# A modulation stage rewritten: plain fp32 products of raw weight blocks in four column groups of TensorE

## The reference, cut to what matters

```python
def ada_modulation(c, w_ada, b_ada):
    return jnp.split(jax.nn.silu(c) @ w_ada + b_ada, N_MOD, axis=-1)

def trunk_layer(x, c, ...):
    shift1, scale1, gate1, shift2, scale2, gate2 = ada_modulation(c, w_ada, b_ada)
    h = modulate(rms_norm(x, g_norm1), shift1, scale1)      # h * (1 + scale) + shift
    ...                                                     # attention, S5, output projection, PEER experts
```

## Time and profile before

| | us |
|---|---|
| median of 3 runs | 5242.03 (5230.54 to 5265.98) |
| the profiled execution, its own time | 5261.86 |
| its span, first to last instruction | 5260.2 |
| end of the modulation products in that span (`scale1` is made) | 394.92 |

### The profile page before, as it was taken

The page is one execution under the profiler, slowest core; times in us unless marked ns, Lnnn a source line. Parts: engine busy times, 40 slices in busy tenths (PEclk is TensorE's granted clock), DMA queues, the critical chain, the costliest instruction groups (busy, mean ns, idle before and its releaser), DMA issues. The chain is left out here.

```text
span 5260.2 us, 58810 instructions
## 1 busy us (share of the span) xinstructions
PE 4319.6 (82%) x23026; PEld 3825.3 (73%) x23026; DVE 2787.5 (53%) x4247; ACT 1426.3 (27%) x1507; POOL 536.8 (10%) x461
## 2 busy tenths in 40 slices
PE   4677998674447989235499999999999999999997
PEld 2227997463336979234499999999989888888896
DVE  4663223316663232699744444444456667666675
ACT  4553112101232131057522222222222222222222
POOL 0000000005300000044300000000000000000000
PEclk8888998766678999667799999999999999999998
DMA  6762221222203222112476666666667667666764
GB/s 246 304 253 73 87 80 53 90 74 43 66 31 134 81 99 95 53 56 96 152 261 236 236 233 232 237 236 233 233 241 272 228 251 255 242 247 238 256 244 160
DMA packets 219977, 912.23 MB, mean 173 GB/s; under 512 B 23138, under 2 KB 111586, under 8 KB 137650
## 3 DMA queue, kind: packets, MB, share of 16 engines
q1 hardware_dynamic: 178018, 641.51, 33.8%
q0 software_dynamic: 37376, 268.52, 14.6%
q10 hardware_dynamic: 4432, 0.20, 0.1%
HBM read 818.10 MB, written 87.87 MB: 172 GB/s over the span
## 5 line engine op out<-in xcount | busy, mean ns | idle before, releaser
L2269 DVE TENSOR_TENSOR part_lo<-raw,part_hi 128x2048 fp32r<-128x2048 f32 x128 | 293.4, 2292 | 464.3 <-ACT part_hi L2191 464.3
L2191 ACT ACTIVATE part_hi<-raw 128x2048 fp32r<-128x2048 f32 x128 | 245.3, 1917 | 1050.4 <-PE ps_u L2231 489.7
L2269 DVE TENSOR_TENSOR h_lo<-raw,h_hi 128x2048 fp32r<-128x2048 f32 x128 | 293.4, 2292 | 388.6 <-ACT h_hi L2191 387.7
L2191 ACT ACTIVATE h_hi<-raw 128x2048 fp32r<-128x2048 f32 x128 | 245.3, 1916 | 925.0 <-PE ps_u L2231 475.8
L2246 PE MATMUL ps_v<-h_hi,part_hi 128*128 128x448 f32 x1024 | 384.6, 376 | 46.3 <-issue 41.0
L2231 PE MATMUL ps_u<-h_hi,part_hi 128*128 128x448 f32 x1024 | 378.0, 369 | 19.4 <-DVE part_lo L2269 19.4
L2246 PE MATMUL ps_v<-h_lo,part_hi 128*128 128x448 f32 x1024 | 382.2, 373 | 0.0
L2246 PE MATMUL ps_v<-h_hi,part_lo 128*128 128x448 f32 x1024 | 382.0, 373 | 0.0
L2231 PE MATMUL ps_u<-h_lo,part_hi 128*128 128x448 f32 x1024 | 377.8, 369 | 0.0
L2231 PE MATMUL ps_u<-h_hi,part_lo 128*128 128x448 f32 x1024 | 377.7, 369 | 0.0
L2231 PE MATMUL ps_u<-h_hi 128*128 128x448 f32 x1024 | 376.8, 368 | 0.0
(11 more groups left out here) (389 smaller groups left out, 9020.5 us busy)
## 6 DMA issues: line engine op xcount, KB each, us to landing
raw<-in_uT SPq DMA_DIRECT2D x128, 1024.0 KB
raw<-in_vT SPq DMA_DIRECT2D x128, 1024.0 KB
qkvu<-in_w_ada SPq DMA_DIRECT2D x48, 2048.0 KB, 8.3
w_raw<-in_w_in SPq DMA_DIRECT2D x32, 1024.0 KB
wo_raw<-in_w_out_q SPq DMA_DIRECT2D x32, 1024.0 KB, 4.9
gates_scratch<-gate_blk SPq DMA_DIRECT2D x14, 2048.0 KB, 7.5
a_scratch<-wt SPq DMA_DIRECT2D x128, 224.0 KB, 1.9
at<-a_scratch SPq DMA_DIRECT2D x16, 1792.0 KB, 7.6
```

The source lines that it names most:

```text
L2191: act.activation(hi[n % 2], raw[n % 2][:].rearrange("p (k c) -> p k c", k=KC), ACT.Copy).then_inc(hi_done, 1)
L2269: dve.tensor_tensor(lo[n % 2], raw[n % 2][:].rearrange("p (k c) -> p k c", k=KC), hi[n % 2].bitcast(F32), ALU.subtract).then_inc(lo_done, 1)
```

## The change

Only `modulate` changes, and one small constant input, `pick`, is added. The weights are no longer split. PE multiplies the raw fp32 halves as they land, as plain fp32. `c` has one set of columns: `c_cols`, 9 columns of silu(c) and 23 of zeros for each chunk. Chunk k's product is written to PSUM partitions 32*(k % 4) and on, so the 16 chunks of a block fall into four column groups with four partial sums. ACT copies all 128 x 512 partial sums; the turning is a plain fp32 product of that copy (as stationary operand, 128 columns at a time) with `pick`, a 128 x 9 matrix that adds the four groups; DVE adds the bias in one operation. The raw halves lie in a ring of four buffers, and SP reloads a buffer when PE has used it (`half_used`). All loops are written out instead of run as hardware loops. The diff, cut to its core:

```diff
-        raw = [free[:, u * KC * WB:(u + 1) * KC * WB].rearrange("p (k c) -> p k c", k=KC) for u in range(2)]
+        raw = [free[:, u * KC * WB // 2:(u + 1) * KC * WB // 2].rearrange("p (k c) -> p k c", k=KC // 2) for u in range(NR)]
...
+        c_cols = sb("c_cols", [P, KC, CG_])
+        pick = sb("pick", [P, NC_])
...
-        row = [sb(f"row{u}", [2 * NC_, WB]) for u in range(2)]
+        row = [sb(f"row{u}", [P, WB]) for u in range(2)]
...
-                for f in range(2):
-                    if not isinstance(n, int):
-                        sp.wait_ge(lo_done[f], n - 1)
...
+            def load(n):
+                if n >= NR:
+                    sp.wait_ge(half_used, n - NR + 1)
+                sp.dma_start(raw[n % NR].rearrange("p k c -> p (k c)"), w_ada[n // 2, n % 2]).then_inc(w_full[n % NR], 16)
+
+            load(0)
+            load(1)
             sp.dma_start(x[:], I["xT"].rearrange("(k p) t -> p k t", p=P)).then_inc(x_in, 16)
...
+            for n in range(2, 2 * NBLK):
+                load(n)
+
+        @block.gpsimd
+        def _(pool):
+            pool.memset(c_cols[:], 0.0).then_inc(cleared, 1)
...
+            act.dma_start(pick[:], I["pick"]).then_inc(small_in, 16)
+            act.wait_ge(small_in, 64)
+            act.wait_ge(cleared, 1)
+            act.activation(c_cols[:, :, 0:NC_], c_in[:], ACT.Silu).then_inc(silu_done, 1)
...
-            def high_parts(n, u, f):
-                act.wait_ge(w_full[u][f], 8 * (n - u) + 16)
-                act.wait_ge(used[f], n)
-                act.activation(w_hi[f], raw[u][:, f * KH:(f + 1) * KH, :], ACT.Copy).then_inc(hi_done[f], 1)
...
+            for n in range(NBLK):
+                act.wait_ge(half_used, 2 * n + 2)
+                if n >= 2:
+                    act.wait_ge(mod_t, n - 1)
+                act.activation(row[n % 2][:], ps_row[n % 2][:], ACT.Copy).then_inc(row_copied, 1)
...
+            def rows(n):
+                if n >= 2:
+                    pe.wait_ge(row_copied, n - 1)
                 for f in range(2):
-                    pe.wait_ge(lo_done[f], n + 1)
-                    for k in range(KH):
-                        for w in (w_hi, w_lo):
-                            mm = pe.matmul(ps_row[u][0:2 * NC_, :], c_two[:, f * KH + k, :], w[f][:, k, :],
...
+                    i = 2 * n + f
+                    pe.wait_ge(w_full[i % NR], 16 * (i // NR + 1))
+                    for k in range(KC // 2):
+                        g, part = k % CT, f * (KC // 2) + k
+                        mm = pe.matmul(ps_row[n % 2][g * CG_:(g + 1) * CG_, :], c_cols[:, part, :], raw[i % NR][:, k, :],
+                                       start=part < CT, stop=part >= KC - CT)
+                    mm.then_inc(half_used, 1)
+
+            def turn(n):
+                pe.wait_ge(row_copied, n + 1)
+                if n >= 2:
+                    pe.wait_ge(mod_done, n - 1)
+                for j in range(JB):
+                    mm = pe.matmul(ps_mod[n % 2][:, j * NC_:(j + 1) * NC_], row[n % 2][:, j * P:(j + 1) * P], pick[:],
+                                   start=True, stop=True)
+                mm.then_inc(mod_t, 1)
+
+            rows(0)
...
+            for n in range(1, NBLK):
+                rows(n)
+                turn(n - 1)
+            turn(NBLK - 1)
...
-            def low_parts(n, u, f):
-                dve.wait_ge(hi_done[f], n + 1)
-                dve.tensor_tensor(w_lo[f], raw[u][:, f * KH:(f + 1) * KH, :], w_hi[f].bitcast(F32),
-                                  ALU.subtract).then_inc(lo_done[f], 1)
...
+    a["pick"] = np.concatenate([np.eye(32, NC_, dtype=np.float32)] * 4)
```

More of the change, by code:

```diff
@@ L123, in modulate @@
     ps = lambda n, s, d=F32: ctx.enter_context(nc.psum_tensor(n, s, d))
-    KH = KC // 2
+    NBLK = NMOD * P // WB
+    CT, CG_ = 4, 32
+    KT = KC // CT
+    NR = 4
+    JB = WB // P
     with ctx:
@@ L146, in modulate @@
         ps_mod = [ps(f"ps_mod{u}", [P, 512]) for u in range(2)]
-        x_in, small_in, w_full = sem("x_in"), sem("small_in"), [[sem(f"ada_full{u}{f}") for f in range(2)]
-                                                                        for u in range(2)]
-        silu_done, c_hi_done, c_lo_done = sem("silu_done"), sem("c_hi_done"), sem("c_lo_done")
+        x_in, small_in, w_full = sem("x_in"), sem("small_in"), [sem(f"ada_full{u}") for u in range(NR)]
+        cleared, silu_done = sem("c_cleared"), sem("silu_done")
         sq_done, sq_used, norm_sum, std_done = (sem(n) for n in ("sq_done", "sq_used", "norm_sum", "std_done"))
[L152 to L157, removed]
+        half_used, row_copied, mod_t, mod_done = (sem(n) for n in ("ada_used", "row_copied", "mod_t", "mod_done"))
         xn_done, scale_done, h_prompt, h_sample = (sem(n) for n in ("xn_done", "scale_done", "h_prompt", "h_sample"))
         hin_done = sem("hin_hi_done"), sem("hin_lo_done")
-        held = sem("ada_held")
         v_step = sem("mod_v_step")
-        NA = NMOD * P // WB // 2
         block = ctx.enter_context(nc.Block())
[L165 to L180, removed]
         @block.sync
@@ L204, in _ @@
             act.dma_start(g1[:], I["g1T"]).then_inc(small_in, 16)
[L205 to L218, removed]
-            def high_parts(n, u, f):
-                act.wait_ge(w_full[u][f], 8 * (n - u) + 16)
-                act.wait_ge(used[f], n)
-                act.activation(w_hi[f], raw[u][:, f * KH:(f + 1) * KH, :], ACT.Copy).then_inc(hi_done[f], 1)
[L225 to L230, removed]
+            act.dma_start(pick[:], I["pick"]).then_inc(small_in, 16)
+            act.wait_ge(small_in, 64)
+            act.wait_ge(cleared, 1)
+            act.activation(c_cols[:, :, 0:NC_], c_in[:], ACT.Silu).then_inc(silu_done, 1)
+            act.wait_ge(x_in, 16)
+            for c in range(KC):
+                if c >= 2:
+                    act.wait_ge(sq_used, c - 1)
+                act.activation(sq[c % 2][:], x[:, c, :], ACT.Square).then_inc(sq_done, 1)
+            act.wait_ge(norm_sum, 1)
+            act.activation(halves(std[:]), fold(ps_norm), ACT.Sqrt, scale=1.0 / D, bias=C["eps"][:, 0:1]
+                           ).then_inc(std_done, 1)
+            for n in range(NBLK):
[3 more added lines that the diff above has]
+                act.activation(row[n % 2][:], ps_row[n % 2][:], ACT.Copy).then_inc(row_copied, 1)
             act.wait_ge(scale_done, 1)
@@ L244, in _ @@
         def _(pe):
[L245 to L255, removed]
@@ L270, in turn @@
[L270 to L286, removed]
@@ L287, in _ @@
-            turn(NA - 1, 0)
-            rows(2 * NA - 1, 1)
-            turn(NA - 1, 1)
+            pe.wait_ge(silu_done, 1)
+            def rows(n):
+                if n >= 2:
+                    pe.wait_ge(row_copied, n - 1)
+                for f in range(2):
+                    i = 2 * n + f
[5 more added lines that the diff above has]
+                    mm.then_inc(half_used, 1)
@@ new lines, in turn @@
+            def turn(n):
[7 more added lines that the diff above has]
+            rows(0)
+            for c in range(KC):
+                pe.wait_ge(sq_done, c + 1)
+                for a in range(2):
+                    mm = pe.matmul(ps_norm[:, a, 0:HT], C["ones"][:], sq[c % 2][:, a * HT:(a + 1) * HT],
+                                   start=(c == 0), stop=(c == KC - 1))
+                if c < KC - 1:
+                    mm.then_inc(sq_used, 1)
@@ L303, in keep @@
[L303 to L310, removed]
@@ L312, in norm, with keep @@
-            def norm():
-                dve.wait_ge(std_done, 1)
-                step(dve.reciprocal(rstd[:], std[:]))
-                for c in range(KC):
-                    ins = dve.tensor_tensor(x[:, c, :], x[:, c, :], rstd[:], ALU.mult)
-                    if c == KC - 1:
-                        ins.then_inc(xn_done, 1)
-                    else:
-                        step.mark(ins)
-                dve.wait_ge(small_in, 48)
-            lagging(dve, low_parts, keep, norm)
-            for u in range(2):
-                dve.wait_ge(mod_done[u], NA)
+            def keep(n):
+                dve.wait_ge(mod_t, n + 1)
+                dve.tensor_tensor(mod[:, JB * n:JB * n + JB, :], ps_mod[n % 2][:, 0:JB * NC_].rearrange(
+                    "p (j r) -> p j r", j=JB), bc(b_ada[:, JB * n:JB * n + JB], 2, [P, JB, NC_]), ALU.add
+                    ).then_inc(mod_done, 1)
@@ L326, in _ @@
+            dve.wait_ge(small_in, 64)
+            dve.wait_ge(std_done, 1)
+            step(dve.reciprocal(rstd[:], std[:]))
+            for c in range(KC):
+                ins = dve.tensor_tensor(x[:, c, :], x[:, c, :], rstd[:], ALU.mult)
+                if c == KC - 1:
+                    ins.then_inc(xn_done, 1)
+                else:
+                    step.mark(ins)
+            for n in range(NBLK):
+                keep(n)
+            dve.wait_ge(mod_done, NBLK)
             dve.wait_ge(xn_done, 1)
```

24 lines of the change are left out of this document (1 added, 23 removed).

## The result

The changed kernel takes 5078.0 us in the median (5051.8 to 5098.8) against 5242.0; the ratio is 0.967, with a 95% interval of 0.9642 to 0.9698. The forecast was 5133.5 with a range of 5105 to 5190. The profiled execution has a span of 5050.1 us, against 5260.2.

What follows compares the result with a forecast made beforehand. An ACT-DVE-PE chain was taken as the modulation stage's bound, transfers as the next. Start, norm and 42 loads (218.6 us) put `scale1` at 286.4 instead of 394.92: 108.5 us off 5242.03 gives 5133.5, range 5105 to 5190.

Steps and rivals of the forecast that it cites:

- the bound and its successor: Modulation stage: a chain ACT, DVE, PE takes 13.68 us a block; transfers, 10.4 us a block, are the next bound.
- the first rival: Modulation stage: column groups don't run side by side, PE binds, `scale1` at 401 to 421 us, total 5257; chance 0.12.
- the rate: Modulation stage's weight loads: 403 GB/s, so loads 6 to 47 take 42 x 5.204 = 218.6 us.
- the overlap: Products in the modulation stage: half the possible overlap, 6.8 us a block, between 3.4 (four at a time) and 13.6 (none).
- `pick`: Stage start: silu waits for this extra small transfer, taken as 0.8 us more, bounds 0 and another 12 us.
- Slower transfers: Modulation stage's loads run at 357 GB/s, 5.87 us each; the gain is 80 us, total 5162; chance 0.10.
- Bare weight loads: PE loads weights only while no product runs: 19.1 us a block, 112 us slower, total 5354; chance 0.04.
- nothing behind it changes: a barrier follows, then the same code.: Everything after the modulation stage, including the experts' stage, was taken to keep its time.
- the 12 waits "for nothing visible": PE's 41.0 us of waits in the experts' stage, at most 4.7 each: upper bound for code fetches, covered by queued loads.

Runs made afterwards that it cites:

- half_products: Changed kernel with only 8 of each block's 16 chunks multiplied, all weights still loaded; `scale1` at 271.91 us, 2.8 us earlier, at 427 GB/s.
- two_groups: Changed kernel with two column groups instead of four; `scale1` at 278.75 us, 4.1 us later, rate still 427 GB/s.
- one_group: Changed kernel with all products of a block in one column group; 5217.4 us, 0.9943 of the kernel before, `scale1` at 408.9 us.
- The pads: Do-nothing PE instructions ahead of the modulation stage: 128 in the kernel before (5196.8 us against 5243.6), 129 in the changed kernel (5135.3 against 5077.2).
- after_pad129: Changed kernel with 129 do-nothing instructions ahead of the modulation stage's work on PE; 5135.3 us against 5077.2 for the changed kernel run again.

## Why the prediction was right in the stage and wrong in the time

**Right: the bound and its successor.** The chain through the three engines set 13.68 us a block, and without it the transfers do; half_products and two_groups show it. Also right was the price of the first rival: no overlap was put at 401 to 421 us for `scale1`, and one_group measured 408.9.

**Mis-sized, in the stage (11.7 us): the rate.** 403 GB/s was taken from the stage's first 15 us, but over the 42 loads behind the norm it was 427. These are the rows of the stage's start in the trace after:

```profile
34.20 0.34 ACT L184 ACTIVATE c_cols<-c_in 128x144 f32<-128x144 f32 x1 [14.73 <-DMA pick<-in_pick]
34.59 6.54 PE L220 MATMUL ps_row<-qkvu,c_cols 128*32 128x512 f32 x32 [34.59 <-ACT c_cols L184]
57.27 3.64 PE L220 MATMUL ps_row<-qkvu,c_cols 128*32 128x512 f32 x32
```

Half 2 is used up at 57.27 + 1.9 = 59.2 us (59.3 in the sum), and the last half's first product starts at 268.96. Less the 2.1 us of latency a load took 4.94 us and not 5.20: 42 x 0.26 = 11 us. The start runs at 403 to 404 GB/s in both kernels; that the small transfers of ACT's queue lie beside it there would explain it, and was not tested.

**Mis-sized, and cancelled: the overlap and `pick`.** I took two records at a time, the second of one product beside the first of the next. Four run at a time, which took block 0 from 9.15 us to 6.5 and half 2 from 3.4 to 1.9. Against it the wait for `pick` put silu at 34.2 instead of 30.2, 4 us more than taken and within the bounds that I gave. That these cancel to 0.1 us is luck.

"Slower transfers" fell with all of this. The Trainium skill ("DMA: Bandwidth & Descriptors", Specifications) gives about 358 GB/s as the limit of a core's share of the HBM; this kernel's trace, of one core, does not agree, as it holds 427 GB/s from 70 to 260 us. "Bare weight loads" fell too: a step of 0.43 us holds a bunch of loads that takes 0.13 and records that need 0.426 alone, so the loads run beside them. By the Trainium skill's rule ("TensorE: Matmul & The Clock Gate", Part 3, The mechanism), that a weight load overlaps running products only where its row group differs, they could not; the trace does not agree.

By the stage alone the median would have come to about 5122 us, within the range.

**Wrong: "nothing behind it changes: a barrier follows, then the same code."** This term stood in the sum at nothing. The instructions are the same, but they lie elsewhere, and in the kernel before the place was a bad one. The pads price it at 47 to 58 us; with the stage's 120 that makes 167 to 178, where the gain is 164 (158 to 188 by its interval). The row that gave it away stood in the forecast: the 12 waits "for nothing visible" of the earlier trace rows. I read them as an upper bound for what a code fetch costs inside the rewritten stage and looked for cover there. They were the place where fetches already cost something, in a loop whose code had only to move by 128 instructions, and a diff that writes out loops moves all code behind it by some 1660. No row told the sign: a shift can as well cost 58 us, as after_pad129 shows. What could be seen beforehand is that such waits exist, in pairs at the turns of a loop, and that the diff changes the length of PE's program; the range should have had some 50 us for that on both sides.

The profiled spans make the second cause look larger than it is. Of their 90 us in the experts' stage 24 are the first pass's rate and 6 that of two stretches in the second; about 60 are the refetched loop. Nor is the slower rate a trait of the kernel before: its profiled executions, padded or not, have it in the first pass, but so have some of the changed kernel's variants (1271 to 1272 us), and the 119.6 us between the kernels in the quiet place leave no room for it.

## What to carry to other kernels

When a chain of engines sets the pace, work out what the next bound allows (here 4 MB at the rate of an undisturbed stretch) and how far each part stays below it; what goes beyond, such as the third and fourth column group, only turns into waiting. When a diff changes how many instructions an engine has, look at its other loops for waits without a releaser at their turns, and count the packets of the code queue in them: a loop that is fetched in every turn can become one that is not, or the reverse, and filling instructions in an idle place test it cheaply. Judge a saving in one stage at that stage's own mark, if the rest of the kernel scatters by more.

## What the runs showed of the hardware that I had not expected

- TensorE's code for a loop of about 1600 instructions is fetched once (12 packets of 16 KB over the pass) or in each of the seven turns (67 packets), by where it begins. In the second case PE waits 18 to 42 us in the pass, up to 4.7 us at a time, and starts again at the low clock: at 4132.69 us a record of the kernel before took 0.74 us behind a wait of 3.29, twice the usual 0.37.
- A stream of fp32r products of 448 columns runs at one of two rates at the full clock, a start every 0.2027 or every 0.2067 us. The rate holds until PE pauses and may be the other behind a pause; a pass of 6144 products without one takes 1247 to 1248 or 1271 to 1272 us. For one and the same pass it differs between executions of one program. What picks it stays open.
- Plain fp32 products in four column groups run four records at a time: 16 records of 512 columns in 1.92 us, where one group needs 13.92 us for 32. Their weight loads, in bunches of four, lie beside the running products.
